# Expert rows of a mixture-of-experts layer are added straight into the two outputs

## The reference, cut to what matters

```python
x = x + (ga * y_a + gb * y_b) @ w_out
x = x + moe(rmsnorm(x, norm2_g), ...)      # shared expert + 8 routed experts a token
# routed part:
ys = lax.map(expert_block, (row_tok, block_e))          # swiglu of a block of rows of one expert
out = jnp.zeros((M + 1, D)).at[row_tok].add(ys * row_w[:, None])   # summed by token
# y_prompt (1, 1024, 1024) and y_sample (8, 1, 1024)
```

## Time and profile before

| | us |
|---|---|
| median of three runs | 2391.46 |
| profiled execution, its own time | 2384.22 |
| profiled execution, span of the trace | 2382.4 |
| PE busy | 2177.4 (91%) |
| DVE busy | 1093.8 (46%) |
| POOL busy | 878.7 (37%) |
| ACT busy | 746.7 (31%) |
| mean granted TensorE clock | 0.945 of full speed |

### The profile page before, as it was taken

One profiled execution on the slowest core, in us unless ns is written; L12 is line 12 of the kernel. 1 busy time (PEld: TensorE's weight loads), 2 busy tenths in 40 slices (PEclk: granted clock), 3 DMA queues, 4 the chain that ended last, 5 costly groups with the idle time before them and its releaser, 6 DMA issues. The chain is left out here.

```text
span 2382.4 us, 36557 instructions
## 1 busy us (share of the span) xinstructions
PE 2177.4 (91%) x13258; PEld 1762.3 (74%) x13258; DVE 1093.8 (46%) x1856; ACT 746.7 (31%) x1233; POOL 878.7 (37%) x824
## 2 busy tenths in 40 slices
PE   7999799878499997999899879999999999999994
PEld 6777677667344446898777638898898899899893
DVE  4487678767376762111257523333333333333331
ACT  6222122245266662111233102332323233233231
POOL 2111222122466660111006603455455555545542
PEclk9999899958699998999999899999999999999997
DMA  6587610064345528984262048999999999999996
GB/s 219 170 270 241 226 35 30 29 193 119 113 147 173 154 68 279 304 278 146 80 217 90 22 174 285 323 329 317 321 326 323 318 326 321 321 324 325 320 316 168
DMA packets 180333, 520.56 MB, mean 219 GB/s; under 512 B 22907, under 2 KB 78866, under 8 KB 153790
## 3 DMA queue, kind: packets, MB, share of 16 engines
q1 hardware_dynamic: 133654, 366.37, 44.8%
q0 software_dynamic: 36208, 93.16, 15.5%
q10 hardware_dynamic: 10368, 59.73, 7.5%
HBM read 442.31 MB, written 125.08 MB: 238 GB/s over the span
## 5 line engine op out<-in xcount | busy, mean ns | idle before, releaser
L2270 PE MATMUL pG_e<-xT,w_e 128*128 128x160 f32 x4224 | 627.5, 302 | 2.0 <-issue 1.3
L2270 PEld LDWEIGHTS pG_e<-xT,w_e 128*128 128x128 f32 x4224 | 586.8, 197 | 29.0 <-issue 25.5
L2370 DVE TENSOR_TENSOR w_e_lo<-w_e,w_e_hi 128x2048 fp32r<-128x2048 f32 x66 | 151.4, 2294 | 338.2 <-ACT w_e_hi L2317 338.2
L565 PE MATMUL pP<-wring,hT_hi 128*128 128x512 f32 (+2 forms) x576 | 228.7, 397 | 21.6 <-DVE wring L500 12.8
L2219 POOL DMA_INDIRECT x_scratch<-y_e,target x66 | 106.9, 1619 | 334.3 <-ACT y_tail L2337 334.3
L566 PE MATMUL pP<-wring,hT_hi 128*128 128x512 f32 (+2 forms) x576 | 223.4, 388 | 0.0
L567 PE MATMUL pP<-wring,hT_lo 128*128 128x512 f32 (+2 forms) x576 | 223.1, 387 | 0.0
L2317 ACT ACTIVATE w_e_hi<-w_e 128x2048 fp32r<-128x2048 f32 x66 | 126.1, 1911 | 277.6 <-DMA w_e<-in_w_e_down 277.6
L2360 DVE COPY xT<-pX 128x512 f32<-128x512 f32 x132 | 90.8, 688 | 233.4 <-PE pX L2254 233.4
L341 POOL TENSOR_TENSOR wring<-turned,wring 128x512 fp32r<-128x512 f32 (+1 forms) x43 | 69.4, 1647 | 228.9 <-ACT wring L375 228.8
L1495 PE MATMUL pG<-hg_hi,wg_hi 128*128 128x344 f32 x384 | 130.3, 339 | 16.7 <-DVE hg_lo L1556 16.7
(11 more groups left out here) (290 smaller groups left out, 4002.8 us busy)
## 6 DMA issues: line engine op xcount, KB each, us to landing
w_e<-in_w_e_gate SPq DMA_DIRECT2D x66, 1024.0 KB, 8.3
w_e<-in_w_e_up SPq DMA_DIRECT2D x66, 1024.0 KB, 12.9
w_e<-in_w_e_down SPq DMA_DIRECT2D x66, 1024.0 KB, 6.9
turned<-in_cache_sb_kv SPq DMA_DIRECT2D x256, 256.0 KB, 3.1
out<-in_cache_win_kv ACTq DMA_DIRECT2D x8, 4094.0 KB
turned<-in_w_in ACTq DMA_DIRECT2D x56, 256.0 KB, 6.2
turned<-in_w_in SPq DMA_DIRECT2D x16, 512.0 KB, 9.1
out<-in_cache_win_kv ACTq DMA_DIRECT2D x8, 1022.0 KB
```

The costliest lines, as they stand in the source:

```text
L565: pe.matmul(pP[:m, i % 4, :w], hi, w_hi(u), start=(c == 0), stop=False)
L2270: last = pe.matmul(pG[:, k, f * BLK:(f + 1) * BLK], wv[:, c, f, :], xT[:, r, c, :], start=(c == 0), stop=(c == KC - 1))
L2370: dve.tensor_tensor(wlo[:, r, :], w[:, r, 2, :], whi[:, r, :].bitcast(F32), ALU.subtract).then_inc(wlo_ready, 1)
```

## The change

Four things change together.

- The shared expert's sums go to the two outputs and no longer to x2, and x2's padding rows are no longer zeroed.
- Each block's results are added to the outputs by four indirect transfers: rows and quarters into the prompt output, rows and quarters into the sample output. Each has a bound: an index above it is out of bounds, and its row is left out. The sample's indices are the token's number with bit 1024 flipped (for quarters bit 4096), so that a prompt token lies above the sample's bound and a sample token above the prompt's. Padding lies above both.
- `y` and `y_tail` have two buffers, so `put` waits for the scatters of two blocks earlier. The scatters into one output still wait for those of the block before into the same output.
- `phase_finish` is gone.

```diff
-        phase_finish(nc, a, o, scratch)
...
-                sp.dma_start(sc["x2"][T:, :]...zero...).then_inc(zero_out, 16)
...
-                        sp.dma_start(sc["x2"][u * P:u * P + m, :], x2[:m, u % 2, :]).then_inc(x2_out[u % 2], 16)
+                        dst = o[0][0, u * P:u * P + m, :] if u < NT - 1 else o[1][:, 0]
+                        sp.dma_start(dst, x2[:m, u % 2, :]).then_inc(x2_out[u % 2], 16)
...
+                dve.tensor_scalar(slot_info[:, :, 4], slot_info[:, :, 0], S, None, ALU.bitwise_xor).then_inc(slots_ready, 1)
+                dve.tensor_scalar(slot_info[:, :, 5], slot_info[:, :, 1], QT * S, None, ALU.bitwise_xor).then_inc(slots_ready, 1)
+                dve.wait_ge(slots_ready, 6)
...
-        target = sb("target", [P, 2, 4], I32)
+        target = sb("target", [P, 2, 6], I32)
-        y = sb("y_e", [P, D])
-        y_tail = sb("y_tail", [P, QW])
+        y = sb("y_e", [P, 2, D])
+        y_tail = sb("y_tail", [P, 2, QW])
...
                     pool.wait_ge(y_copied, it * (2 * U) + 2 * (j + 1))
-                    if seen(it, j, 1):
-                        pool.wait_ge(y_out, it * (U * 32) + 32 * j)
-                    pool.nop(nofuse=True)
-                    pool.indirect_dma_start(sc["x2"], ...target[:, r, 0:1]..., y[:, :], None, compute_op=ALU.add).then_inc(y_out, 16)
-                    pool.indirect_dma_start(x2_quarters, ...target[:, r, 1:2]..., y_tail[:, :], None, compute_op=ALU.add).then_inc(y_out, 16)
+                    for added, rows_to, quarters_to, count, c in ((prompt_added, prompt_out, prompt_quarters, S, 0),
+                                                                  (sample_added, sample_out, sample_quarters, NS, 4)):
+                        if seen(it, j, 1):
+                            pool.wait_ge(added, it * (U * 32) + 32 * j)
+                        pool.nop(nofuse=True)
+                        pool.indirect_dma_start(rows_to, ...target[:, r, c:c + 1]..., y[:, r, :], None,
+                                                bounds_check=count - 1, oob_is_err=False, compute_op=ALU.add).then_inc(added, 16)
+                        pool.indirect_dma_start(quarters_to, ...target[:, r, c + 1:c + 2]..., y_tail[:, r, :], None,
+                                                bounds_check=QT * count - 1, oob_is_err=False, compute_op=ALU.add).then_inc(added, 16)
...
                 def put(it, j):
-                    if seen(it, j, 1):
-                        act.wait_ge(y_out, it * (U * 32) + 32 * j)
+                    if seen(it, j, 2):
+                        act.wait_ge(prompt_added, it * (U * 32) + 32 * (j - 1))
+                        act.nop(nofuse=True)
+                        act.wait_ge(sample_added, it * (U * 32) + 32 * (j - 1))
...
-def phase_finish(nc, a, o, sc):
```

More of the change, by code:

```diff
@@ L103, in build @@
         expert_row = sb("expert_row", [1, NBLK + 1], I32)
-        slot_info = sb("slot_info", [P, NBLK, 4], I32)
+        slot_info = sb("slot_info", [P, NBLK, 6], I32)
         with ExitStack() as attention:
@@ L1750, in _ @@
                 sp.dma_start(sc["h2"][T:, :].rearrange("(p n) d -> p n d", n=5), zero.unsqueeze(1).broadcast_to([BLK // 5, 5, D])).then_inc(zero_out, 16)
-                sp.dma_start(sc["x2"][T:, :].rearrange("(p n) d -> p n d", n=5), zero.unsqueeze(1).broadcast_to([BLK // 5, 5, D])).then_inc(zero_out, 16)
                 sp.wait_ge(fill_set, 1)
@@ L1773, in _ @@
                     sp.wait_ge(stored[i], 32 * len(range(i, NT, 2)))
-                sp.wait_ge(zero_out, 32)
+                sp.wait_ge(zero_out, 16)
                 sp.wait_ge(mlo_ready, NT)
@@ L1926, in _ @@
                         if b == 1:
-                            act.wait_ge(zero_out, 32)
+                            act.wait_ge(zero_out, 16)
                         if b >= 2:
@@ L2128, in phase_experts @@
     h2_quarters = sc["h2"].rearrange("t (q n) -> (t q) n", q=QT)
-    x2_quarters = sc["x2"].rearrange("t (q n) -> (t q) n", q=QT)
+    assert S & (S - 1) == 0 and T + BLK <= 2 * S
+    prompt_out, sample_out = o[0][0], o[1][:, 0]
+    prompt_quarters = prompt_out.rearrange("t (q n) -> (t q) n", q=QT)
+    sample_quarters = sample_out.rearrange("t (q n) -> (t q) n", q=QT)
     w_views = [a[n][0].rearrange("e (p c) f -> e p (c f)", p=P) for n in ("w_e_gate", "w_e_up", "w_e_down")]
@@ L2154, in phase_experts @@
         rows_in = [sem(f"e_rows_in{i}") for i in range(2)]
-        y_out = sem("e_y_out")
+        prompt_added = sem("e_prompt_added")
+        sample_added = sem("e_sample_added")
         index_ready = sem("e_index_ready")
@@ L2215, in scatter @@
                     pool.wait_ge(y_copied, it * (2 * U) + 2 * (j + 1))
-                    if seen(it, j, 1):
-                        pool.wait_ge(y_out, it * (U * 32) + 32 * j)
-                    pool.nop(nofuse=True)
[L2219 to L2222, removed]
+                    for added, rows_to, quarters_to, count, c in ((prompt_added, prompt_out, prompt_quarters, S, 0),
[3 more added lines that the diff above has]
+                        pool.nop(nofuse=True)
+                        pool.indirect_dma_start(rows_to, bass.IndirectOffsetOnAxis(ap=target[:, r, c:c + 1], axis=0), y[:, r, :], None,
+                                                bounds_check=count - 1, oob_is_err=False, compute_op=ALU.add).then_inc(added, 16)
+                        pool.indirect_dma_start(quarters_to, bass.IndirectOffsetOnAxis(ap=target[:, r, c + 1:c + 2], axis=0), y_tail[:, r, :], None,
+                                                bounds_check=QT * count - 1, oob_is_err=False, compute_op=ALU.add).then_inc(added, 16)
                 def body(it, old):
@@ L2238, in _ @@
                         scatter(last - (LAG - 1 - n), j)
-                pool.wait_ge(y_out, last * (U * 32) + U * 32)
+                pool.wait_ge(prompt_added, last * (U * 32) + U * 32)
+                pool.nop(nofuse=True)
+                pool.wait_ge(sample_added, last * (U * 32) + U * 32)
                 pool.nop(nofuse=True)
@@ L2333, in put @@
                     act.wait_ge(target_ready, it * U + (j + 1))
-                    if seen(it, j, 1):
-                        act.wait_ge(y_out, it * (U * 32) + 32 * j)
-                    act.activation(y[:, :], pY[:, :], ACT.Copy, scale=scale[:, j % 2, 2:3]).then_inc(y_copied, 1)
-                    act.activation(y_tail[:, :], pQ[:, :QW], ACT.Copy, scale=scale[:, j % 2, 3:4]).then_inc(y_copied, 1)
+                    r = j % 2
+                    if seen(it, j, 2):
+                        act.wait_ge(prompt_added, it * (U * 32) + 32 * (j - 1))
+                        act.nop(nofuse=True)
+                        act.wait_ge(sample_added, it * (U * 32) + 32 * (j - 1))
+                    act.activation(y[:, r, :], pY[:, :], ACT.Copy, scale=scale[:, r, 2:3]).then_inc(y_copied, 1)
+                    act.activation(y_tail[:, r, :], pQ[:, :QW], ACT.Copy, scale=scale[:, r, 3:4]).then_inc(y_copied, 1)
                 def body(it, which):
```

## The result

The changed kernel is slower by about 1%. Its median is 2417.22 us (2415.01 to 2420.03, 4 runs) against 2391.93 us (2384.79 to 2392.54, 4 runs) of the kernel before: a ratio of 1.0115, with a 95% interval of 1.0093 to 1.0138. The profiled execution took 2415.01 us with a span of 2412.9 us, 30.5 us more than before. The forecast was 2375 us, with a range of 2362 to 2432. The measured time lies in that range only because it had been drawn wide for rival 2, dearer bounded transfers, and that rival was not what happened.

The account below looks back on a forecast made before the run. PE was taken to bound the kernel at 13.81 us a block, with POOL at 13.5. From 2384.22, less 15.4 for the end, plus 0.6 and 1, came 2370.4, put at 2375 for the runs' median; range 2362 to 2432.

Parts of the forecast that it names:

- rival 2: POOL's loop: bounded transfers are dearer to issue, deciding from 0.24 us each; slower, span 2455 at 0.5 each; chance 0.22.
- POOL's packed block: POOL's shortest expert block, its issues, gaps and copies added without waiting for anyone: 11.8 us, bounds 11.6 to 12.1.
- The size of the hindrance: What DVE's subtraction takes from POOL in a block: 1.7 us taken, 1.4 by the means, 2.29 at most.
- The gap before the sample pair: POOL's gap ahead of the sample's two scatters: between 0.30 and 0.80 us, taken as 0.5.
- The formula 1509 + 61 P: Span if POOL's period P binds the expert stage; it passes PE's 2367 only at P = 14.07; 13.5 expected.
- ACT's removed wait: ACT's 2.7 us a block for the previous block's scatters to land; removing it is worth nothing in the expert stage.
- The skipped padding: 22% of the scattered bytes go, about 0.14 MB a block; worth nothing, as PE waits for no transfer.
- the bound's price: Extra issue time on POOL for each of the four bounded scatters: taken as zero to 0.1 us each.
- Rival 1: POOL's loop: POOL is fully hindered by the subtraction, period 14.4 us, span 2387, no change; chance 0.10.
- Rival 3: POOL's sample pair is nearly free: P near 12, end 3 us sooner, 2367 own time; chance 0.64 together with the forecast.
- A sign that I had named: POOL's scatters: the forecast is wrong if a bounded transfer lasts over 1.85 us.
- The end: After PE's last product: with no copy following the last scatters, the span ends near 2367, saving 15.4 us.

Follow-up runs that it names:

- e5: The changed kernel with DVE computing the low part of the down weights behind the block's hidden rows, not ahead; ratio 1.0047 to the kernel before.
- e4: The kernel before with two buffers for y and y_tail alone; ratio 0.9990 to the kernel before.
- e8: The changed kernel with one buffer for y and y_tail, so ACT waits for both scatter pairs of the block before; ratio 1.1083 to the kernel before.
- e11: The kernel before with a bound on its two scatters into the scratch tensor, leaving out padding; ratio 0.9989 to the kernel before.
- e6: The changed kernel with target copy ahead of the gather, and down-weight rounding and subtraction behind the same block's hidden rows; ratio 0.9941 to the kernel before.
- e1: The changed kernel with POOL copying a block's target columns ahead of the gather, no longer behind it; ratio 0.9994 to the kernel before.
- e3: The changed kernel without the sample's pair of scatters and the waits on them; ratio 0.9912 to the kernel before.
- e7: The changed kernel with DVE computing the low part of only half of the down weights; ratio 0.9939 to the kernel before.
- e9: The changed kernel with down-weight rounding and subtraction behind the hidden rows, target copy left behind the gathers; ratio 1.0011 to the kernel before.

## Why the prediction was wrong, point by point

**The step that failed** is in the sum for POOL's packed block: "target 0.19; and 0.80 for the wait on that copy". I took y as copied by then. But ACT waits for the same target copy before it scales y, so the place of the 0.80 is 2.65 us: 0.2 to start, 1.5 for the two copies, 0.9 to wake POOL. The wait stood in the code before, and in the earlier trace rows POOL waits 4.58 us for ACT right behind the target copy; I read that as spare time that PE and the landing made. For the kernel before this was right, for ACT was then kept by a landing. When POOL's four scatters used up that time, the target copy became what ACT waits for last. I asked what each added wait would do, and did not ask which old wait would end last once POOL is late.

**The size of the hindrance** was somewhat high, 1.7 assumed against 1.15 measured and 0.9 in e5; the whole subtraction would have been 2.29. But I took it as spread over the block at random. The subtraction follows the copy of y in ACT's order, as do the scatters in POOL's, so each block meets it at the same place. With both terms right the sum is 13.35 + 1.15 = 14.5. The gap before the sample pair is 0.30, the lower bound, not 0.5.

**The formula 1509 + 61 P** gives 2396 at 14.54, and 2399 at 14.59, which is the mean over the 61 blocks it counts; the span was 2412.9. The last four blocks take 44.1 us, not 34.0, since the turn with ACT is in each of them too (2355.87 to 2399.94 in POOL's timeline of the changed kernel); the way from the last block's first scatter to the end is 13.0, not 11.2; and 1.8 lie ahead of the stage.

**What was right.** PE bound the kernel, and a period over PE's passes straight into the time. ACT's removed wait was worth nothing in the stage before (e4), though with four scatters the second buffer is needed: without it the changed program takes 1.108 times what the kernel before takes, and with it 1.012 (e8). The skipped padding and the bound's price are nil (e11), so rival 2, the slower one, was the wrong mechanism for the right direction. Rival 1, a POOL over PE's period with the subtraction inside it, was half of the truth, with the other half missing. Rival 3 fell too: a pair with nearly all rows skipped costs POOL as much as a full one (1.55 and 1.55 in POOL's rows above). A sign that I had named, a bounded transfer of over 1.85 us, did appear (2.71 us), but the subtraction made it and not the bound.

**The end, which I called nearly certain,** was worth less than forecast. From PE's last product on I had 16.4 us left; it is 19.7 in the changed kernel and 19.4 in e6, so against the 32.0 of before 12.3 to 12.6 us are saved, not 15.4. The last block's first scatter comes 6.7 us behind PE's last product, not 5.2. The last scatter lands 2.9 us after its issue, sooner than my 4.9, but behind the landing stand 4.4 us and not 0.4: I had read the 0.4 off the end of `phase_finish`, and now POOL ends the kernel (last section).

**What I had not seen at all** is the second chain. Rounding and subtracting the down weights stand ahead of the hidden rows in the order of ACT and DVE. In the kernel before the hidden rows were ready 1.2 us (median of 1640:2340) before PE's next gate product began, and 0.2 in the tightest block. Rounding waits for the down load; that it starts 0.6 us later in the median, and 1.2 at most, uses this up in a third of the blocks (e1). Why the load comes later is open. The sample pair goes with it, for rounding starts at 6.6 us after the load's issue without the pair (e3) and at 7.2 to 7.5 with it (e7, e1), but where the transfers meet was not tried.

## What to carry to other kernels

When an engine gets more work, list every engine that waits for anything that it produces, small copies included, and put its new lateness into each of those waits; a wait covered by another today becomes a turn in a loop tomorrow. Issue small copies on which others wait ahead of the long work in the same order, not behind it. When a run shows that one engine holds up another, note where in the period it does so: here the same subtraction cost 1.15, 0.9, 0.55 or nothing, by what began beside it. And an operation that isn't needed for a block's own critical product (here the split of weights used a block later) belongs behind that product in an in-order engine, for its slack is otherwise no larger than the product's.

## What the runs showed of the hardware that was not expected

A bounded scatter with adding costs POOL the same 1.55 to 1.62 us whether all rows are in bounds or nearly none, and a skipped row is still a small transfer: packets under 512 bytes rose from 22907 to 49247 in the changed kernel.

The subtraction holds up a scatter that begins beside it, and not one that is under way. In e9 the scatter of 2017.04 ran beside the subtraction of 2017.31 for 1.31 us and took 1.58; the next began inside it and ended 1.43 us behind it (2018.93 + 2.10 against 2017.31 + 2.29). Over the traces of all runs, 354 scatters were under way when a subtraction began, and they took 1.55 to 1.77 us. Of 283 that began inside one (with over 0.15 us of it left) all but one, which began only 0.01 us behind its start, ended 1.42 to 1.48 us behind its end. A free scatter takes 1.55 to 1.62, so by these rows about 0.1 us of it passes before it is held; that is an estimate. Nor is the subtraction held up by a scatter under way: it takes 2.28 to 2.30 us in all 66 blocks of the changed kernel.

Behind the last landing POOL still has an instruction of 4.15 us, which the view of its line shows with its duration in ns (least, median, most) and its start in us:

```profile
L2180 POOLq DRAIN  x1: 4146/4146/4146, 2408.5 to 2408.5; - x1
```

The last scatter was issued at 2405.53, so it landed within 2.9 us, and the kernel ends 4.4 us behind that. In e3, with one pair, the same instruction takes 3.65 us, and in the kernel before too, where `phase_finish` came behind it: landed at 2363.1, first copy issued at 2367.1. What the removal of the copy can give therefore ends at this instruction.
